# First MLP of a two-block transformer in two phases, and the second layer's modulation moved into the projection

## What is computed

```python
for i in range(DEPTH):                       # DEPTH = 2
    sh1, sc1, g1, sh2, sc2, g2 = modulation(cond_lat, ada_w[i], ada_b[i])   # c @ ada_w[i]: 1024 x 6144
    u = modulate(h, sh1, sc1)
    if i % 2 == 0:
        p = u @ w_in[j]                      # projection: conv part (3 x 512 columns), q, k, v
        o = diff_attention_blocks(q, k_all, v_all, lam)
        y = concatenate([conv_mixer(p[..., :COL_CONV], conv_w[j]), sub_ln(o, ...)]) @ w_out_mix[j]
    else:
        y = fourier_mix(u) @ w_out_fourier[j]
    h = post_norm_residual(h, y, g1, ln_g[i, 0], ln_b[i, 0])
    h = post_norm_residual(h, sq_relu_mlp(modulate(h, sh2, sc2), mlp_w1[i], mlp_w2[i]), g2, ...)

def sq_relu_mlp(u, w1, w2):
    return jnp.square(jax.nn.relu(u @ w1)) @ w2
```

## Time and profile before

| What | us |
|---|---|
| Median of 3 runs | 3121.57 |
| Lowest and highest run | 3121.11, 3122.23 |
| Span of the profiled execution | 3123.9 |
| Projection, V and convolution units (173.2 to 352.8) | 179.6 |
| mlp0 (667.5 to 1355.4) | 687.9 |
| Odd part of the Fourier mix (1355.4 to 1390.3) | 34.9 |
| mlp1 (1525.9 to 2165.2) | 639.3 |

### The profile page before, as it was taken

One profiled execution on the slowest core, in us unless ns is written; L12 is line 12 of the kernel. 1 busy time (PEld: TensorE's weight loads), 2 busy tenths in 40 slices (PEclk: granted clock), 3 DMA queues, 4 the chain that ended last, 5 costly groups with the idle time before them and its releaser, 6 DMA issues. The chain is left out here.

```text
span 3123.9 us, 36049 instructions
## 1 busy us (share of the span) xinstructions
PE 3016.0 (97%) x14139; PEld 2476.2 (79%) x14139; DVE 2237.8 (72%) x2938; ACT 1309.7 (42%) x1963; POOL 638.9 (20%) x567
## 2 busy tenths in 40 slices
PE   6999999999999999999999999999898999999998
PEld 2888888878888888878788877887777788888887
DVE  4716488586677777585787788787697777778575
ACT  4411387363333333342643333337427553333334
POOL 0010335244344434040421120002000112120000
PEclk9999999999999999999999999999999999999999
DMA  7426321212332232211144475432111225457432
GB/s 242 145 84 212 86 80 55 99 48 83 100 101 82 95 103 99 75 37 48 68 164 149 149 282 206 149 101 69 41 55 55 95 98 182 149 197 281 172 102 101
DMA packets 213843, 369.94 MB, mean 118 GB/s; under 512 B 14599, under 2 KB 125818, under 8 KB 213674
## 3 DMA queue, kind: packets, MB, share of 16 engines
q1 hardware_dynamic: 176474, 240.02, 23.5%
q0 software_dynamic: 28848, 97.21, 8.3%
q10 hardware_dynamic: 8352, 30.41, 2.7%
HBM read 284.75 MB, written 82.84 MB: 118 GB/s over the span
## 5 line engine op out<-in xcount | busy, mean ns | idle before, releaser
L687 PE MATMUL psum<-U_hi,page_r 128*128 128x512 f32 x1660 | 656.6, 396 | 24.3 <-DVE U_lo L698 12.9
L688 PE MATMUL psum<-U_lo,page_r 128*128 128x512 f32 x1660 | 648.1, 390 | 0.0
L689 PE MATMUL psum<-U_hi,page_r 128*128 128x512 f32 x1660 | 647.8, 390 | 0.0
L687 PE MATMUL psum<-page_r,act_page_r 128*128 128x512 f32 x1272 | 496.1, 390 | 4.7 <-DVE page_r L698 4.7
L688 PE MATMUL psum<-page_r,act_page_r 128*128 128x512 f32 x1272 | 495.4, 389 | 0.0
L689 PE MATMUL psum<-page_r,act_page_r 128*128 128x512 f32 x1216 | 473.7, 390 | 0.0
L698 DVE TENSOR_TENSOR page_r<-page,page_r 128x1024 fp32r<-128x1024 f32 (+1 forms) x184 | 233.9, 1276 | 249.9 <-ACT page_r L693 245.0
L687 PEld LDWEIGHTS psum<-U_hi,page_r 128*128 128x128 f32 x1660 | 312.6, 188 | 102.1 <-DVE U_lo L698 21.4
L689 PEld LDWEIGHTS psum<-U_hi,page_r 128*128 128x128 f32 x1660 | 312.6, 188 | 66.4
L688 PEld LDWEIGHTS psum<-U_lo,page_r 128*128 128x128 f32 x1660 | 312.9, 189 | 62.2
L693 ACT CAST page_r<-page 128x1024 fp32r<-128x1024 f32 (+1 forms) x218 | 214.7, 989 | 318.1 <-PE psum L689 125.9
(11 more groups left out here) (417 smaller groups left out, 5444.1 us busy)
## 6 DMA issues: line engine op xcount, KB each, us to landing
d_act_mlp<-page POOLq DMA_DIRECT2D x222, 256.0 KB, 3.8
act_land<-d_act_mlp SPq DMA_DIRECT2D x108, 512.0 KB, 3.7
page<-in_mlp_w_dram SPq DMA_DIRECT2D x68, 512.0 KB, 4.3
page<-in_ada_w_dram SPq DMA_DIRECT2D x48, 512.0 KB, 4.8
page<-in_w_in_dram SPq DMA_DIRECT2D x38, 512.0 KB, 4.1
pair_raw<-in_mlp_w_dram SPq DMA_DIRECT2D x14, 1024.0 KB, 5.6
pair_raw<-in_w_up_dram SPq DMA_DIRECT2D x14, 1024.0 KB, 5.4
ada_land<-in_ada_w_dram ACTq DMA_DIRECT2D x24, 512.0 KB, 4.7
```

The source lines that it names most:

```text
L687: pe.matmul(out, l_hi, r_hi, start=start, stop=False, skip_group_check=read_between)
L688: pe.matmul(out, l_hi, r_lo, start=False, stop=False, skip_group_check=read_between)
L689: return pe.matmul(out, l_lo, r_hi, start=False, stop=stop, skip_group_check=read_between)
```

## The change

**What it does.** mlp0 goes through `pe_two_phase` as the other two MLPs do; `pe_mlp` and everything that fed it (block planning, POOL's sums, the late modulation tiles) is gone. All 48 tiles of the second layer's modulation are loaded and summed in the projection, and the tiles of groups 3 to 5 of the first layer move ahead within it. How many tiles lie beside each of the twelve convolution weights is a table, and two more say after which tile of V and after which convolution unit a column sum stands. At post0 the token tiles are taken in the folding order, so that mlp0's halves are already those of the Fourier fold. The seam from mlp0 to the Fourier mix is written anew for an MLP that ends with a down product (`act_fold_seam`, `dve_fold_seam`), and the gate row of layer two is turned inside that last down product.

```diff
-TWO_PHASE = ("mlp1", "mlp2")
-GATE_OF = {"mlp1": (1, 1)}
+TWO_PHASE = ("mlp0", "mlp1", "mlp2")
+GATE_OF = {"mlp0": (0, 1), "mlp1": (1, 1)}
...
             for part in (1, 2, 0):
                 up(w_in, part * D_CONV + i * P)
-                ada_units(2)
+                ada_units(ADA_BESIDE_CONV[3 * i + (1, 2, 0).index(part)])
...
+ADA_BESIDE_CONV = (24, 6, 5, 4, 5, 4, 4, 4, 4, 4, 4, 4)
+ADA_SUM_AFTER_V = {3: (0, 3), 6: (0, 4), 9: (0, 5)}
+ADA_SUM_AFTER_CONV = {1: (1, 0), 2: (1, 1), 3: (1, 2), 5: (1, 3), 6: (1, 4), 10: (1, 5)}
...
+    if i == MOD_AT and (layer, part) in MOD_BEFORE:
+        dve_mod(k, dve, on, *MOD_BEFORE[layer, part])
...
         m.then_inc(*k.up_done.inc("v", t))
+        if t in ADA_SUM_AFTER_V:
+            pe_ada_sum(k, pe, on, *ADA_SUM_AFTER_V[t])
...
-            if m in (2, 6):
-                pe_ada_sum(k, pe, on, 0, 3 + m // 6, (k.row_b, k.row_g)[m // 6])
-    pe_ada_sum(k, pe, on, 0, 5, k.row_b)
+            if m in ADA_SUM_AFTER_CONV:
+                pe_ada_sum(k, pe, on, *ADA_SUM_AFTER_CONV[m])
...
-        self.order = FOLD_ORDER if fourier else tuple(range(TT))
+        self.order = FOLD_ORDER if name in ("post0", "post1") else tuple(range(TT))
...
-    Boundary("post1", ("mlp0", BLOCKS - 1), (0, 1), False, None, None, False, fourier=True),
+    Boundary("post1", "mlp0", (0, 1), False, None, None, False, fourier=True),
...
+def dve_fold_seam(k, dve, on, name, b):
+
+    measure = lambda which, t: dve_norm_measure(k, dve, on, b, which, t)
+    scale = lambda which, t: dve_norm_scale(k, dve, on, b, which, t)
+
+    def post(n):
+        dve_down_add(k, dve, on, name, len(DOWN_ORDER) - 1, n - TPC)
+        measure("post", n)
+
+    at = k.first["table"]
+    scale("pre", TPC - 1)
+    dve_weights(k, dve, on, at)
+    dve_odd_fold(k, dve, on, 0)
+    post(4)
+    dve_odd_low(k, dve, on, 0)
+    dve_odd_fold(k, dve, on, 1)
+    scale("post", 4)
+    post(5)
+    dve_odd_low(k, dve, on, 1)
+    scale("post", 5)
+    dve_weights(k, dve, on, at + 1)
+    post(6)
+    scale("post", 6)
+    measure("pre", 4)
+    scale("pre", 4)
+    post(7)
+    scale("post", 7)
+    dve_gain(k, dve, on, b, 7)
+    measure("pre", 5)
+    scale("pre", 5)
+    measure("pre", 7)
+    dve_odd_fold(k, dve, on, 2)
+    measure("pre", 6)
+    scale("pre", 6)
+    scale("pre", 7)
+    dve_odd_low(k, dve, on, 2)
+    dve_odd_fold(k, dve, on, 3)
```

More of the change, by code:

```diff
@@ L778, in dve_mod, with pe_gate_row @@
     m.then_inc(*k.mod_ok.inc(layer, part))
-def pe_gate_row(k, pe, on, layer, which):
-    banks = [k.banks.take(on, ("gate", layer, which, i), (k.gate_ok, (layer, which))) for i in range(2)]
+def pe_gate_row(k, pe, on, layer, which, slots=(None, None)):
+    banks = [k.banks.take(on, ("gate", layer, which, i), (k.gate_ok, (layer, which)), slot=slots[i]) for i in range(2)]
     for i in range(KT):
@@ L1033, in dve_turn_chunk @@
             between(i)
-STASHED = {"post2": "mlp1", "pre4": "mlp2"}
+STASHED = {"post0": "mlp0", "post2": "mlp1", "pre4": "mlp2"}
 def stash_of(k, c, i):
@@ L1046, in stash_free @@
     else:
-        on.wait_ge(*k.pe_done.at("even", KT - 1))
+        if stage == "post0":
+            on.wait_ge(*k.lo.at("u", "heads", NCH - 1, HEADS - 1))
+        else:
+            on.wait_ge(*k.pe_done.at("even", KT - 1))
         if c:
@@ L1812, in behind @@
     def behind(self):
-        return self.down[0] if self.down[0] in TWO_PHASE else None
+        return self.down if self.down in TWO_PHASE else None
     def by_pool(self, tt):
-        return tt in self.order[:self.on_pool] and not (self.behind and tt < TPC)
+        return tt < self.on_pool and not (self.behind and tt < TPC)
     @property
@@ L2235, in pool_boundary @@
 def pool_boundary(k, pool, on, b):
[L2236 to L2237 removed]
+    for t in filter(b.by_pool, range(TT)):
+        h = b.h(k, t)
         on.wait_ge(*k.normed.at(b.name, t))
@@ L2797, in down_source, with down_tile @@
     return k.page[:, ODD_PAGE[d]:ODD_PAGE[d] + 2, half, :]
-def down_tile(i, t):
+TILES_OF = {"mlp0": FOLD_ORDER, "mlp1": tuple(range(TT)), "mlp2": tuple(range(TT))}
+def down_tile(name, i, t):
     rows, cols = QUARTER[DOWN_ORDER[i]]
-    return (1 - rows) * TPC + t, cols
+    return TILES_OF[name][(1 - rows) * TPC + t], cols
 def pe_down_product(k, pe, on, name, i, after=None):
@@ L3414, in dve_two_phase @@
                 gate("17"[i - 5], 1, d)
+        if name == "mlp0" and i == FIRST_DONE - 1:
+            dve_gate_row(k, dve, on, 1, 0)
+    if after and after.fourier:
+        dve_fold_seam(k, dve, on, name, after)
+        return
     if after:
@@ L3449, in pool_two_phase @@
         if n > PLAIN:
-            for what in ("12",) + sums:
+            store("12", n - 1)
+            store("S1", n - 1)
+        if n > PLAIN:
+            for what in sums[1:]:
                 store(what, n - 1)
```

720 lines of the change are left out of this document (157 added, 563 removed).

## The result

The changed kernel takes 3139.59 us, the median of four runs (3137.87 to 3142.24). The kernel before took 3121.9 beside it (3121.11 to 3126.33). The ratio is 1.005, with an interval of 1.0036 to 1.0064: slower by half a per cent, where 3113.0 was forecast and the range ended at 3130. The profiled execution of after took 3142.24 us. The kernel before was measured again beside each later group of tests and took 3126.8, 3125.3 and 3125.2 us there (medians); after was not. So a test's ratio stands against the kernel before, and what a test changes against after is read from the stages of the profiles.

A forecast was written before the change was run, and what follows sets the result against it. The prediction took TensorE, busy 97% of the time, to bound the kernel. Its terms, -46.5 + 10.2 + 22.7 + 7.3 - 2.3 = -8.6 us, took 3121.57 to 3113.0 us, range 3098 to 3130.

The forecast's parts named there:

- Term 1: mlp0, with the pause ahead of it, would take 641.4 us in place of 687.9: -46.5 us.
- (b): mlp0 after its first three up tiles: mlp1's 616.3 us, adjusted for transposes and gate row to 613.8.
- Term 2: In the projection, six more column sums on TensorE at 1.7 us each: +10.2 us.
- Term 3: In the projection, TensorE waits 20.7 us for modulation tiles at three sums, plus 2 us of slow clock: +22.7 us.
- The first of the three release times: In the projection, the last tile for the sum after convolution unit 2 is ready at about 273 us.
- rival B: In the projection, the ring of three pages is slower, 2.39 us a load, 16 us more: 3129.3 us; chance 0.15.
- Term 4: Seam from mlp0 to the Fourier mix: third odd low part 28.4 us after the start, not 20.1; +7.3 us.
- six measurings ..., 17.7 us: At the seam, VectorE's passes from six measurings through the third fold and its low part take 17.7 us.
- the bound 12: At the seam, the upper bound of the added time, 12 us, if the two bank waits lengthen too.
- Term 5: At mlp1's start, the three up tiles take 20.7 us in place of 23.0: -2.3 us.
- A: In the projection, the ring of three pages is faster, 1.58 us a load, tiles hidden: 3090.3 us; chance 0.10.
- C: The seam after mlp0 hides itself, third low part at 20 us as before, nothing added: 3105.7 us; chance 0.11.

The follow-up runs named there:

- reload_order: The changed kernel with mlp0's saved H tiles fetched from DRAM in the order of use; 3130.76 us, ratio 1.0013 to the kernel before.
- few_mod_tiles: The changed kernel, loading only the first and last of eight weight tiles for each of the second layer's six modulation column groups; 3108.88 us in one run.
- seam_order: The changed kernel with another order of VectorE's and ScalarE's steps at the seam from mlp0 to the Fourier mix; ratio 1.0035 to the kernel before.
- bank_shift: The changed kernel with the count of PSUM banks moved on by 5 ahead of the mixer's last down tiles; 3144.33 us in one run.
- no_pool_gain: The changed kernel with POOL's gain and shift passes at the seam after mlp0 cut from 1024 columns to 8; 3133.08 us in one run.

## Why the prediction was wrong, step by step

**Term 1, mlp0: right in mechanism and start, short by 8.6.** The pause at the first up tile was put at 8.4 and measured 8.43; the three tiles end 28.4 after the mixer, forecast 27.6, which is 0.8 of the 8.6. The step that failed is (b), "from there to the end, mlp1 takes 616.3": it took mlp1's rows as mlp0's, and did not ask which inputs of that stretch depend on the tile order, which the change also alters. The reload of H did: 621.6 us in place of 613.8, and 613.3 once it was in the order of use.

**Term 2: right.** 10.2 forecast, 9.9 by the run with few tiles.

**Term 3: right in mechanism, 5 us short.** Waits stand at the three sums named, 4.10, 2.37 and 10.67 us against 5.7, 5.9 and 9.1. The sum of the waits, 17.1, is less than the 20.7, but the slow clock costs 10.9 (38.2 less the sums' 10.2 and the waits; TensorE's busy time in the stage is longer by the same), where I had 2. The two trade: a slow TensorE arrives later and waits less. So it is partly luck that the term missed by 5 only: the waits were put 3.6 too high and the clock 8.9 too low. The first of the three release times does not follow from its own terms: 235.9 and 17 loads at 2.05 are 270.8, and the text has 273; measured was 271.9. What counts is when the sum after unit 6 is released, 339.9 against 336.7, and what comes behind. Two of SyncE's rows, both loads of a convolution weight, with 36 loads from the first up to the second:

```profile
253.16 0.37 SPq L639 DMA_DIRECT2D page<-in_w_in_dram  x1
...
334.28 0.38 SPq L639 DMA_DIRECT2D page<-in_w_in_dram  x1
```

That is 81.1 us, 2.25 a load. The forecast has for the same loads 36 x 2.05 and 4.2 for the two passes of the convolution that stand among them, 78.0: the pace is 3.1 us slower, or 0.09 a load, where rival B had 0.34. That is the 3.2 us. The other 2 us are the clock behind the third wait, 0.57 over the sixteen microseconds from 329 and still 0.96 over the next 45; I had allowed 2 us where it took 4. In the four other kernels with the same tables that sum is released between 337.2 and 339.9, so a part of the 5 us is scatter. The rate in the Trainium skill, "DMA: Bandwidth & Descriptors", section Bandwidth, from which the text estimated 1.5 us for 512 KB, would have made the term vanish. It did not: this ring took 2.25 us a load.

**A cost that no term had: the attention's start, +3.3.** The last sum's column (`mod`, L733) is needed right there; TensorE waits 1.56 us where it waited 0.86 before, which is 0.7. The other 2.6 us are the clock: 0.72 over the first 12.4 us, where the kernel before had 1.00. The wait alone does not bring it. In `reload_order`, with the same instructions and the same wait of 1.56 us, it stayed at 1.00:

```profile
388.20:400.60 12.40, 10.84 (x53) 8.85 (x54) 9.07 (x15) 4.01 (x5) 0.00 (x0) 1.00 0.20 46
```

So it did in `few_mod_tiles`; in `seam_order` and `bank_shift` it was 0.72 again, in `no_pool_gain` 0.86, and the mixer column follows (315.3 and 315.2; 317.9; 316.6). What decides it no run tells; it stays open.

**Term 4, the seam: right in mechanism, +8.2.** Its step "six measurings ..., 17.7 us" took every pass at its undisturbed time, and named POOL only as someone who might be early. The lock between VectorE and POOL cost 7.2 us in it. The last 1.1 us is the 1 us that the term took off for a faster clock behind the low part: from there to the even part the two kernels take 14.8 and 14.9 us, both at a granted clock of 0.83. I had written the bound 12 for "if the two bank waits lengthen too", and 15.5 was measured: the bound was too narrow.

**Term 5: right**, -2.8 against -2.3 (639.5 and 636.7 us).

**The rivals.** A did not come: the tiles were not hidden. B, a slower ring, was right in its sign; of its 16 us some 3 came. C did not come: the seam grew. The side of the result, slower, had a chance of 0.13, all but 0.01 of it on the ring; what made the kernel slower in fact was the sum of three places (mlp0 8.6, the projection and the attention's start 8.6, the seam 8.2), of which the reload order, the port lock and most of the slow clock stood in no rival.
